# Dense attention in a ten-layer kernel: two pairs' scores stand among the value slots, and five k tiles of the first two output slots among the last pairs' turns

## The reference, cut to what matters

```python
q, k, v = split(h @ w_qkv)
s = (q @ k.T) * 64 ** -0.5 - slope[head] * (qpos - kpos)
s = where(qpos >= kpos, s, -inf)
p = softmax(s)
out = (p @ v).reshape(L, 1024) @ w_out
x = x + gate * out
```

## Time and profile before

| what | value |
|---|---|
| runs | 1863.86, 1865.82, 1866.27 us (median 1865.82) |
| profiled execution, first to last instruction | span 1865.1 us; its own time is not given apart from this, and the median of the runs lies 0.7 us above the span |
| instructions | 36260 |
| busy: TensorE / its weight loads / VectorE / ScalarE / GpSimd | 97% / 93% / 71% / 51% / 20% of the span |
| granted TensorE clock, mean | 0.994 |
| HBM read | 368.89 MB, 198 GB/s over the span |

### The profile page before, as it was taken

The page is one execution under the profiler, slowest core; times in us unless marked ns, Lnnn a source line. Parts: engine busy times, 40 slices in busy tenths (PEclk is TensorE's granted clock), DMA queues, the critical chain, the costliest instruction groups (busy, mean ns, idle before and its releaser), DMA issues.

```text
span 1865.1 us, 36260 instructions
## 1 busy us (share of the span) xinstructions
PE 1803.1 (97%) x14574; PEld 1733.4 (93%) x14574; DVE 1323.5 (71%) x1824; ACT 948.5 (51%) x1357; POOL 377.5 (20%) x371
## 2 busy tenths in 40 slices
PE   3999999999999999999999999999999999999998
PEld 2999989979999999999889999988999989689998
DVE  6677877888767576768876555897666767866665
ACT  3554555474645465446465445316544533764453
POOL 1222200051222122211143221002222200431221
PEclk9999999999999999999999999999999999999999
DMA  9877835745577647675924554313555533134551
GB/s 376 319 274 279 324 113 181 277 151 226 184 290 264 256 179 293 253 279 177 372 92 161 188 191 180 142 62 114 177 183 180 180 143 133 41 109 167 191 187 67
DMA packets 51059, 371.10 MB, mean 199 GB/s; under 512 B 5664, under 2 KB 5664, under 8 KB 6048
## 3 DMA queue, kind: packets, MB, share of 16 engines
q1 hardware_dynamic: 41760, 302.85, 44.4%
q0 software_dynamic: 9216, 67.11, 9.2%
HBM read 368.89 MB, written 1.05 MB: 198 GB/s over the span
## 4 chain that ended last, share of the span: by engine, by line
PE 83%; DVE 10%; ACT 4%; issue 1%; DMA 1%; POOL 0%; POOLq 0%; SPq 0%; DVEq 0%; ACTq 0%
PE gu L721 39%; PE acc L729 8%; PE acc L728 8%; PE acc L730 8%; DVE arena L2424 3%; PE gu L1054 2%; PE gu L1193 2%; PE gu L728 2%; PE gu L730 2%; PE gu L729 2%; DVE w_lo L1876 2%; DMA mring<-in_mods 1%; DVE mring L1891 1%; DVE arena L2166 1%; PE acc L1264 1%
## 5 line engine op out<-in xcount | busy, mean ns | idle before, releaser
L1876 DVE TENSOR_TENSOR w_lo<-ring,w_hi 128x2048 fp32r<-128x2048 f32 x265 | 613.7, 2319 | 271.6 <-ACT w_hi L1442 271.5
L1442 ACT ACTIVATE w_hi<-ring 128x2048 fp32r<-128x2048 f32 x265 | 504.9, 1907 | 74.6 <-PE acc L730 49.3
L721 PE MATMUL gu<-Hs_hi,w_hi 128*128 128x258 f32 (+1 forms) x2112 | 427.8, 284 | 2.5 <-DVE Hs_lo L1940 1.3
L721 PE MATMUL gu<-Hs_lo,w_hi 128*128 128x258 f32 (+1 forms) x2112 | 423.1, 282 | 0.0
L721 PE MATMUL gu<-Hs_hi,w_lo 128*128 128x258 f32 (+1 forms) x2112 | 422.5, 281 | 0.0
L651 POOL TENSOR_TENSOR arena<-arena,rstd 128x512 f32<-128x512 f32 x132 | 201.0, 1523 | 831.1 <-ACT arena L1456 778.4
L721 PEld LDWEIGHTS gu<-Hs_hi,w_hi 128*128 128x128 f32 x2112 | 325.7, 189 | 4.8 <-issue 1.8
L721 PEld LDWEIGHTS gu<-Hs_hi,w_lo 128*128 128x128 f32 x2112 | 325.8, 189 | 0.0
L721 PEld LDWEIGHTS gu<-Hs_lo,w_hi 128*128 128x128 f32 x2112 | 325.4, 189 | 0.0
L729 PE MATMUL acc<-hid_lo,w_hi 128*128 128x256 f32 x1056 | 297.8, 282 | 0.0
L728 PE MATMUL acc<-hid_hi,w_hi 128*128 128x256 f32 x1056 | 296.4, 281 | 1.2 <-DVE hid_lo L2095 1.2
(11 more groups left out here) (413 smaller groups left out, 2841.5 us busy)
## 6 DMA issues: line engine op xcount, KB each, us to landing
ring<-in_weights SPq DMA_DIRECT2D x276, 1024.0 KB, 4.8
mring<-in_mods POOLq DMA_DIRECT2D x64, 1024.0 KB, 6.1
mring<-in_mods SPq DMA_DIRECT2D x8, 1024.0 KB, 7.5
con<-in_constants SPq DMA_DIRECT2D x1, 1408.0 KB, 12.1
X<-in_x SPq DMA_DIRECT2D x1, 1024.0 KB, 7.2
out<-X SPq DMA_DIRECT2D x1, 1024.0 KB, 3.9
cact<-in_c SPq DMA_DIRECT2D x1, 512.0 KB, 3.3
vec<-in_vectors SPq DMA_DIRECT2D x1, 498.0 KB, 4.1
```

Source lines behind the costliest of these rows:

```text
L721: ins = mm(dst, part, x_lo if i == 1 else x_hi, start=start and i == 0, stop=stop and i == 2, skip_group_check=True)
L1442: act.activation(w_hi[buffer_of(n0, s)][:, :], ring[:, n % RING, :], ACT.Copy).then_inc(hi_ready, 1)
L1876: dve.tensor_tensor(w_lo[b][:, :], ring[:, n % RING, :], w_hi[b][:, :].bitcast(F32), ALU.subtract).then_inc(split_ready, 1)
```

## The change

It puts the scores of pair 0 behind slot 9 and those of pair 1 behind slot 10 (HEAD_START = 2), with VectorE's mask and maximum ahead of the lower parts of slots 12 and 13 and ScalarE's exponentials behind the upper parts of these slots; the exponential's table is loaded after slot 8's evacuation. The two pairs' buffers move off H_lo, and the filler matmuls of turns 0 and 1 go. VectorE now waits for the end of slot 11 before the third pair. On TensorE the turns 8 to 11 of `attention` are each followed by k tiles of slots 12 and 13 together: k = 0 and 1, then 2, 3 and 4 (WOVEN). `project_parts` does the other three k of slot 12, then those of slot 13, then slots 14 and 15. The bodies of `score`, `raise_scores`, `normalise` and `mask` are the lines that stood in `attention` before. GpSimd's program is unchanged.

```diff
--- before.py
+++ after.py
         HR = nc.alloc_sbuf_tensor_at("HR", [P, KD * L + 2 * L], F32, offset=h_at)
-        Pb_moba = [HR[:, b * 2 * TRI:(b + 1) * 2 * TRI].rearrange("p (e t) -> p e t", e=2) for b in range(3)]
-        Pb_moba.append(pairs_of(9800, 1)[:, 0])
-        Pb_nsa = [pairs_of(0, 2)[:, b] for b in range(2)] + Pb_moba[0:2]
+        Pb_h = [HR[:, b * 2 * TRI:(b + 1) * 2 * TRI].rearrange("p (e t) -> p e t", e=2) for b in range(2)]
+        Pb_moba = [pairs_of(9800, 2)[:, b] for b in range(2)] + Pb_h
+        HEAD_START = 2
+        WOVEN = ((0, 1), (2,), (3,), (4,))
+        Pb_nsa = [pairs_of(0, 2)[:, b] for b in range(2)] + Pb_h
@@ -801,20 +803,26 @@
...
-            def project_parts(n0, s0, x_hi, x_lo):
+            def project_tile(n0, s0, s, k, x_hi, x_lo):
+
+                for e in range(2):
+                    ins = three(acc[:, s - s0, e * L:(e + 1) * L], buffer_of(n0, s),
+                                slice(k * L + e * P, k * L + (e + 1) * P), x_hi[:, k, :], x_lo[:, k, :],
+                                start=(k == 0 and e == 0), stop=(k == KD - 1))
+                if k == KD - 1:
+                    ins.then_inc(slot_done, 1)
+
+            def project_parts(n0, s0, x_hi, x_lo, done=0, ahead=0):
...
                 for s in range(s0, s0 + 4):
-                    state["split"] += 1
-                    pe.wait_ge(split_ready, state["split"])
-                    for k in range(KD):
+                    if s >= s0 + ahead:
+                        state["split"] += 1
+                        pe.wait_ge(split_ready, state["split"])
+                    for k in range(done if s < s0 + ahead else 0, KD):
                         if s == s0:
                             state["h"] += 1
                             pe.wait_ge(h_ready, state["h"])
...
+                        project_tile(n0, s0, s, k, x_hi, x_lo)
@@ -944,23 +952,27 @@
...
-            def attention(units, base, Pb, out=None):
+            def score(a, u, base):
+
+                both = ((0, slice(0, HD)), (1, slice(HD, P)))
+                if u >= 1:
...
+                ins.then_inc(score_ready, 1)
+
+            def attention(units, base, Pb, started=0, weave=None):
...
-                for u in range(n + LAG + 1):
+                for u in range(started, n + LAG + 1):
                     if u < n:
...
+                        score(units[u], u, base)
                         if u < LAG:
                             for _ in range(4):
@@ -1001,6 +1013,10 @@
...
+                    if weave is not None and u >= n:
+                        if u == n:
+                            pe.wait_ge(mask_done, base["u"] + n)
+                        weave(u - n)
@@ -1032,6 +1048,7 @@
...
+                units = list(pairs_moba())
@@ -1054,10 +1071,25 @@
...
                     ins.then_inc(slot_done, 1)
+                    if 12 - HEAD_START <= s + 1 < 12:
+                        u = s + 1 - (12 - HEAD_START)
+                        score(units[u], u, UNITS["moba"])
...
-                attention(pairs_moba(), UNITS["moba"], Pb_moba)
-                project_parts(n0, 12, O_hi, O_lo)
+
+                def weave(step):
+
+                    if step == 0:
+                        state["split"] += 2
+                        pe.wait_ge(split_ready, state["split"])
+                    for k in WOVEN[step]:
+                        state["h"] += 1
+                        pe.wait_ge(h_ready, state["h"])
+                        for s in (12, 13):
+                            project_tile(n0, 12, s, k, O_hi, O_lo)
+
+                attention(units, UNITS["moba"], Pb_moba, HEAD_START, weave)
+                project_parts(n0, 12, O_hi, O_lo, done=sum(len(w) for w in WOVEN), ahead=2)
@@ -1570,7 +1602,17 @@
...
+            def raise_scores(u, base, Pb):
+
+                act.wait_ge(max_ready, base["u"] + u + 1)
+                b = u % PBUF
+                for e in range(2):
+                    for tt, (c0, c1) in enumerate(((0, P), (P, TRI))):
+                        ins = act.activation(Pb[b][:, e, c0:c1], Pb[b][:, e, c0:c1], ACT.Exp,
+                                             bias=nmax[:, b, tt, e:e + 1], accum_out=psum_[:, b, tt, e:e + 1])
+                ins.then_inc(pexp_ready, 1)
+
+            def attention(units, base, Pb, out=None, started=0):
...
-                for u in range(n + LAG):
+                for u in range(started, n + LAG):
@@ -1666,8 +1702,11 @@
                     evacuate(n0 + j, *dst[j])
                     if j < 11:
                         high(n0, j + 3)
-                act.activation(rtok[:, :], ones[:, 0:2], ACT.Exp)
-                attention(pairs_moba(), UNITS["moba"], Pb_moba)
+                    if j == 8:
+                        act.activation(rtok[:, :], ones[:, 0:2], ACT.Exp)
+                    if 12 - HEAD_START <= j + 1 < 12:
+                        raise_scores(j + 1 - (12 - HEAD_START), UNITS["moba"], Pb_moba)
+                attention(pairs_moba(), UNITS["moba"], Pb_moba, started=HEAD_START)
                 high(n0, 14)
@@ -2263,19 +2302,40 @@
...
+            def mask(a, u, base, Pb):
+
+                b = u % PBUF
+                dve.wait_ge(score_ready, base["u"] + u + 1)
+                if u >= PBUF:
+                    dve.wait_ge(t_done, base["u"] + u - PBUF + 1)
...
+                ins.then_inc(mask_done, 1)
+                dve.wait_ge(mask_done, base["u"] + u + 1)
+                dve.tensor_reduce(nmax[:, b, 0, :], Pb[b][:, :, 0:P], AX_X, ALU.max, negate=True)
+                dve.tensor_reduce(nmax[:, b, 1, :], Pb[b][:, :, P:TRI], AX_X, ALU.max,
+                                  negate=True).then_inc(max_ready, 1)
+
+            def attention(units, base, Pb, out=None, started=0):
@@ -2354,11 +2399,18 @@
...
                 bare_take(2, Q[:, 4:6, :], HD ** -0.5)
+                units = list(pairs_moba())
                 for s in range(5, 14):
+                    u = s - (14 - HEAD_START)
+                    if u >= 0:
+                        mask(units[u], u, UNITS["moba"], Pb_moba)
+                    if u >= 1:
+                        normalise(units[u - 1], u - 1, UNITS["moba"])
                     low(n0, s)
                     fold(5, s - 5)
                 state["free"] += 12
-                attention(pairs_moba(), UNITS["moba"], Pb_moba)
+                dve.wait_ge(slot_done, n0 + 12)
+                attention(units, UNITS["moba"], Pb_moba, started=HEAD_START)
                 low(n0, 14)
```

More of the change, by code:

```diff
@@ L945, in ssm @@
                         spread_root()
-            def attention(units, base, Pb, out=None):
+            def score(a, u, base):
+                both = ((0, slice(0, HD)), (1, slice(HD, P)))
+                if u >= 1:
+                    pe.wait_ge(mask_done, base["u"] + u)
+                for e, rows in both:
+                    mm(acc[:, e, 0:P], a["q"][rows, a["tile"], 0:P], a["k"][rows, a["kt"], 0:P], start=True,
+                       stop=True, skip_group_check=True)
+                for e, rows in both:
+                    ins = mm(acc[:, e, P:TRI], a["q"][rows, a["tile"], P:L], a["k"][rows, a["kt"], :],
+                             start=False, stop=True, skip_group_check=True)
+                ins.then_inc(score_ready, 1)
+            def attention(units, base, Pb, started=0, weave=None):
                 units = list(units)
@@ L1589, in attention @@
                     if u < n:
[L1590 to L1596, removed]
+                        raise_scores(u, base, Pb)
                     if u >= n and out is not None:
@@ L2264, in ssm, with normalise @@
                 state["sq"] += KD
-            def attention(units, base, Pb, out=None):
+            def normalise(a, t, base):
+                b = t % PBUF
+                dve.wait_ge(pexp_ready, base["u"] + t + 1)
+                ins = dve.reciprocal(psum_[:, b], psum_[:, b])
+                if a["gate"] is not None:
+                    link(ins)
+                    c = a["gate"]
+                    ins = dve.tensor_tensor(psum_[:, b], psum_[:, b], gates[:, :, c:c + 4 * NB + 1:4 * NB], ALU.mult)
+                ins.then_inc(norm_ready, 1)
+            def mask(a, u, base, Pb):
[3 more added lines that the diff above has]
+                    dve.wait_ge(t_done, base["u"] + u - PBUF + 1)
+                if a["slope"] is not None:
+                    for e in range(2):
+                        ins = dve.scalar_tensor_tensor(out=Pb[b][:, e, :], in0=cs("dist", 0, TRI),
+                                                       scalar=a["slope"][e], in1=acc[:, e, 0:TRI], op0=ALU.mult,
+                                                       op1=ALU.add)
+                else:
+                    ins = dve.tensor_tensor(Pb[b], acc[:, 0:2, 0:TRI],
+                                            cs("mask_qk", 0, TRI).unsqueeze(1).to_broadcast([P, 2, TRI]), ALU.add)
+                ins.then_inc(mask_done, 1)
[4 more added lines that the diff above has]
```

(5 more changed lines are left out.)

3 lines of the change are left out of this document (1 added, 2 removed).

## The result

The changed kernel has a median of 1869.51 us over 21 runs (1867.29 to 1871.21); the kernel before, run beside it, has 1866.27 us (1863.86 to 1869.0, 21 runs). The ratio is 1.0015 with an interval of [1.0009, 1.0021]: **slower by 2.8 us (1.7 to 3.9)**. That is inside the predicted range and under the 0.2% (3.7 us) that one measurement can tell, though over so many runs the sign is clear. The profiled execution took 1868.88 us for a span of 1867.1; the 1.8 us between them lie around the span. The clock's mean is 0.992 where it was 0.994.

A forecast was written before the change was run, and what follows sets the result against it. It took both TensorE and the VectorE chain starting at slot 12's end to bound the attention layer, with 0.3 us between them. Terms +0.9 +0.5 +0.7 = 2.1 us on 1865.8 gave 1867.9 us, range 1863.2 to 1870.0.

The forecast's parts named there:

- Head start, 2.4 earlier: Attention pairs: scoring pairs 0 and 1 among slots 9 to 11 brings the later turns 2.4 us earlier.
- catch: GpSimd's queue: its last modulation-weight load waits for the last fold, holding pair 0's multiplication until near 927.0.
- Weave, 3.3 more up to slot 12's end: TensorE's last turns: from transpose group 5 to slot 12's end takes 16.3 us instead of 13.0, 3.3 more.
- switches, 0.5: TensorE's woven turns: five uncovered entries and exits cost 0.1 us each, 0.5 in all (0 to 1.0).
- ffn3's first matmul 1.4 later: Behind slot 12: the chain's steps stay unchanged, so ffn3 starts 0.9 + 0.5 = 1.4 us later, at 975.6.
- TensorE idle for 3.8 us: Ahead of ffn3: TensorE ends slot 15 at 971.8 and then stands idle for some 3.8 us.
- Clock, 0.7 (0 to 0.9): ffn3's entry: the idle stand brings a fall of TensorE's granted clock, costing 0.7 us (0 to 0.9).
- Rest, zero: Other attention layer and pair buffers: no queue or instruction moves there, so zero cost.
- TensorE's own chain decides: Rival at the layer's end: folds slip behind, slot 15's end counts, 2.1 to 2.7 us less, 1863.3; chance 0.13.
- It evens out: Rival in the woven turns: waits for O_lo 0 and 1 vanish, clock holds, +0.1 us, 1865.9; chance 0.12.
- The clock does not fall: Rival at ffn3's entry: clock holds, everything else as forecast, 1867.2 us; chance 0.20.
- The clock stays down: Rival at ffn3's entry: low clock spell twice as long, 4.0 us slower, 1869.8; chance 0.13.

The follow-up runs named there:

- e4_folds_in_tail: Changed kernel with the last three modulation folds moved behind VectorE's takes of pairs 4 and 5; median 1866.72 us, ratio 1.0003 against the kernel before.
- e1_head_only: Changed kernel with the head start but without the weave; median 1864.47 us, ratio 0.9986 against the kernel before.
- e11_load_behind: Head start alone, with GpSimd's last load of modulation weights issued behind pair 0's multiplication; median 1865.23 us, ratio 0.9993 against the kernel before.
- e3_slot12_only: Changed kernel with only slot 12's five k among the last turns, slot 13 done whole behind it; median 1865.10 us, ratio 0.9991 against the kernel before.
- e10_changed_again: The changed kernel unaltered, run again in one job with a kernel with filler matmuls; median 1869.19 us, ratio 1.0015 against the kernel before.
- e9_even12: Changed kernel with only slot 12 woven, one k in each of the last four turns; median 1862.82 us, ratio 0.998 against the kernel before.
- e8_folds_later: Changed kernel with the last three folds placed singly behind the takes of pairs 5, 6 and 7; median 1864.52 us, ratio 0.9994 against the kernel before.
- The fillers: Changed kernel with 14 matmuls of zeros behind slot 15, run twice; medians 1867.91 and 1867.96 us, ratios 1.0009 and 1.0008 against the kernel before.
- e2_weave_only: Changed kernel with the weave but without the head start; median 1870.20 us, ratio 1.0018 against the kernel before.

## Why the prediction was right, and where it was not

The sum was +2.1 us (1867.9) and 2.8 (1.7 to 3.9) was measured by the ratio; the median of 1869.51 stands 1.6 above the forecast, of which 0.45 is the kernel before, whose median went from 1865.82 to 1866.27. The mechanism was the forecast one. The layer's 1.60 lies below the sum and the whole time's 2.8 above it, so that the sum came out so near is in part luck.

- **The bound.** Right. The VectorE chain starts at the end of slot 12 and decides; each of its steps has its old length. e4_folds_in_tail shows the other side: with the folds away, TensorE's chain ends the layer.
- **Head start, 2.4 earlier.** Right: 2.27 (copy of transpose 0 and transpose group 5 alike), and 2.28 by e1_head_only. The size came by ScalarE's copy of transpose 0 (930.3 forecast, 930.42 with the shift), and that holds. What did not hold is the name of "catch" for GpSimd's queue. It did keep pair 0's multiplication until its load (the rows stand below), but set nothing; e11_load_behind took that hold away and lost 1.0.
- **Weave, 3.3 more up to slot 12's end, and switches, 0.5.** The sum of the two, 3.8, was 0.26 too large: 3.54 was measured. The waits were predicted as 0.4 and 0.9 and are 0.39 and 0.55, but k = 1 starts where it was put, 4.24 after group 5 (945.25 - 941.01) against 4.35. The 3.57 of slot 13's tiles was the bulk, as e3_slot12_only shows. From k = 1 to slot 12's end the sum without switches had 11.9; it took 12.5, of which 0.2 is the step to ScalarE that the kernel before has too (13.19 against the 13.0 of the sum). That leaves some 0.4 for the switches, an estimate from these rows, within the bounds.
- **ffn3's first matmul 1.4 later.** 1.27.
- **TensorE idle for 3.8 us.** 3.62, ended by VectorE's Hs_lo.
- **Clock, 0.7 (0 to 0.9).** The fall came, at the place named, with 0.70 over 975 to 980. In the layer it cost 0.33, and 0.31 in e10_changed_again: within the bounds and under the 0.7. The slack was put too low. The 48 matmuls take 5.72 where no input is late (e4_folds_in_tail) and 6.96 before, which is 1.24 of slack and not 0.8; the fall itself took 1.57 (7.29 - 5.72), near the 1.7 of the prediction.
- **What the sum has no term for.** 1.27 and 0.33 make 1.60 of the 2.8 (1.7 to 3.9). The other 1.2, as uncertain as the 2.8 itself, is in no row of the layer.
- **Rest, zero.** e1_head_only and e9_even12 give in the whole time what their layers give, within the intervals. For the change itself the layer's 1.60 is just under the interval of the first measurement (1.7 to 3.9) and inside that of e10_changed_again (1.1 to 4.5), so zero is not shown to be wrong, nor right.

GpSimd's timeline in the changed kernel, the counterpart of the earlier trace rows:

```profile
926.22 0.53 POOL L570 DMA_DIRECT2D mring<-in_mods  x1 [6.01 <-DVE mring L1930]
926.76 3.17 POOL L585 TENSOR_TENSOR arena<-arena 128x256 f32<-128x256 f32 x4
...
942.17 0.73 POOL L576 TENSOR_TENSOR O_lo<-arena,O_hi 128x256 fp32r<-128x256 f32 x1
```

The load waits 6.01 for the fold, and pair 0's multiplication follows at 926.76, near the predicted 927.0 (with the shift, 927.2).

Of the rivals, "TensorE's own chain decides" didn't come about here, but its condition was made in e4_folds_in_tail, and then TensorE's chain did decide, though without the gain of 2.1 to 2.7; e8_folds_later, with a smaller collision, comes to it in the layer (2.15). "It evens out" fell, since a wait of 0.94 stayed and the clock fell. "The clock does not fall" fell with the windows. "The clock stays down" is too strong: it is 1.00 again from 980 on.

**Open** is where the 1.2 outside the layer's rows comes from. The fillers point at the clock's fall ahead of ffn3, and the mean clocks (0.992 against 0.994) go with it. Against it: two profiles of the changed kernel show the same fall (7.29 and 7.27 for the 48 matmuls), and e2_weave_only, with the same stand of 3.61 and a fall too, gives 3.4 (1.7 to 5.0) in the whole time for 4.06 in the layer: nothing on top, though the interval leaves room. The rival is the falls elsewhere. Between 1174 and 1186 the clock is 0.86 before and in e2_weave_only, but 0.72 in the changed kernel and in both runs with fillers, and runs of one kernel differ by as much as is to be explained: the kernel before took 1862.99 us at a mean clock of 0.996 and 1868.32 at 0.993. No run separates the two.

## What to carry to other kernels

Filling an engine's gaps with work taken from behind a point is a loss where that point releases the critical chain: put in only the work which that point itself needs (slot 12's k, one per turn, 0.84 us of the layer on top of the head start's 2.28), and leave the next slot's work where it hides the chain. Take the two halves of such a change apart before judging it, since here +4.1 hid -2.3. A gap moved to a place where the engine stands for several microseconds also costs clock; how much of the fall is seen depends on the slack of what follows (here 1.57 became 0.33).

## What the runs showed of the hardware that was not expected

VectorE and GpSimd slow each other down when a fold (two products of 128x1024 in SBUF) runs beside a GpSimd tensor operation. Two multiplications of 128x256 take 2.59 and 4.54 in place of 1.61, one O_lo 1.76 in place of 0.73, and a product of the fold up to 2.05 in place of 1.22. Not every instruction pays: in e4_folds_in_tail the first product beside them took its 1.22. Beside VectorE's masks, which read one of their inputs from PSUM, the multiplication at 929.01 took its 1.61. VectorE's timeline in the kernel before, just ahead of it:

```profile
928.84 1.00 DVE L2294 SCALAR_TENSOR_TENSOR HR<-con,acc 128x384 f32<-128x384 f32 x2
```

The Trainium skill, page "GPSIMD Engine Reference", section "1. Specifications", says that GpSimd shares its SBUF interfaces with VectorE and contends with some of its instructions, those with two SBUF inputs among them. These rows agree, and in them VectorE pays as well. It is why work for VectorE in the tail, where GpSimd makes O_lo, is not free even though VectorE is idle there.
